# VectorE's order in the differential attention: a step's maximum ahead of the output of three steps ago and of the last product

## The chip, the cores and the metric

The kernel runs on one core of a Trainium2 chip. The metric is the device time of one execution in microseconds, the median of several runs; less is better. Four engines compute: TensorE (PE, its weight loads apart as PEld), VectorE (DVE), ScalarE (ACT) and GpSimd (POOL). Each works through its own list of instructions in the order in which the program gives them, and they wait for each other at semaphores.

## What is computed

Two blocks of two layers each stand one after the other, on 512 positions of width 1024, in float32. In each of the first two layers three mixers run side by side over the same normalised input: a neighbourhood attention, a differential attention with four heads, and a convolution. The change touches the differential attention alone:

```python
def blk(qs):
    a, b = qs
    s1 = jnp.einsum('bqhd,bkhd->bhqk', a, k1).astype(jnp.float32) * scale
    s2 = jnp.einsum('bqhd,bkhd->bhqk', b, k2).astype(jnp.float32) * scale
    w = jax.nn.softmax(s1, axis=-1) - lam * jax.nn.softmax(s2, axis=-1)
    return jnp.einsum('bhqk,bkhe->bqhe', w.astype(v.dtype), v)
...
def _diff_merge(o, subln_g, lam_init):
    return (_rms(o, subln_g) * (1.0 - lam_init)).reshape(o.shape[0], o.shape[1], -1)
```

The result is multiplied by a gate and goes into the layer's output projection. 512 latent positions attend to 768 keys (512 latent and 256 of a context). In the first layer the 256 context positions are queries too, and they attend to the 256 context keys alone. The second block (feed-forward layers, a recurrent mixer, a stick-breaking attention) follows and is the longer part of the time.

## The kernel before, in words

Each first-block layer has an `NaStage` (neighbourhood attention) and then a `LateStage` (convolution, differential attention). Once its projections are done, `LateStage` runs a loop over steps. A step is one head and one block of 128 queries. The first layer has 4 x 6 = 24 steps: four heads, each with four latent blocks (768 keys, "full" here) and then two context blocks (256 keys, "short"). The second layer has 4 x 4 = 16 steps, all full.

The work of step k, with the line that the profile gives for it:

- scores, TensorE (L345, 64-row operands): two maps of queries against keys, into one of two sets of three banks of PSUM
- max, VectorE (L1778, `max_dve`): the negated row maxima of both maps, straight from the banks (128x1536 values in a full step, 128x512 in a short one)
- exp, ScalarE (L1708, `exp_act`): two exponentials with their sums
- combine, VectorE (L1786, L1788, L1791, `combine_dve`): a reciprocal, a factor, and then map one minus lambda times map two
- turn, TensorE (L354, 128x128): transposes, two tiles into bank 7 and, in a full step, four into bank 6
- copy, ScalarE (L1695, and L1699 in a full step): out of the banks
- values, TensorE (L345, 128x96): the product with v, into bank 6
- o, VectorE (L1760, `o_dve`): out of bank 6, times the reciprocal of a sum
- root, ScalarE (L1684, L1686, L1688) and norm, VectorE (L1766, `norm_dve`): the RMS norm
- back, TensorE (L354, 128x96): a transpose into bank 7
- fin, VectorE (L1772, `fin_dve`): times the gate

The order on each engine is written out by hand, one line per engine and pass k of its loop, and is skewed over the steps:

- TensorE: values(k-3), back(k-4), turn(k-2), scores(k+1)
- ScalarE: root(k-3), copy(k-2), exp(k)
- VectorE: o(k-3), fin(k-4), max(k), combine(k-1), norm(k-3)

Four waits tie these lists together around the change. max(k) waits for scores(k). o(k-3) waits for values(k-3). turn(k-2) waits for fin(k-4), because bank 7 must be read before it is written again, and its second half waits for o(k-3), because of bank 6. scores(k+1) waits for exp(k-1), which reads the same banks. GpSimd and the DMA queues have nothing to do in the loop except to hold weights that were fetched before.

Of the kernel before, what the change touches and what calls it, by code (L numbers as in the profile page):

```python
# [190 lines left out]
def build(nc, ins, out_dram):  # L191
# [6 lines left out]
    with ctx:  # L198
# [240 lines left out]
        class Norm:  # L439
# [36 lines left out]
            def dve(self, q, e):  # L476
                for s in range(len(spans(self.total))):
                    q.wait_ge(*at(self.tag, "x", "rstd", s))
                    for i, j, c0, c1 in self.each(s):
                        if i >= 3:  # L480
                            q.wait_ge(*at(self.tag, "hi", i - 3))
                            q.wait_ge(*at(self.tag, "lo", i - 3))
                        e.scalar_tensor_tensor(self.full[i % 3][:, 0:c1 - c0], X(j, s), self.gain(j, s),
                                               self.squares.rs[:, c0:c1], MUL, MUL).then_inc(
                            *sig("norm_full", self.tag, "full", i))
                        if i:
                            self.lo(q, e, i - 1)
                self.lo(q, e, i)
# [903 lines left out]
        class LateStage:  # L1392
# [332 lines left out]
            def dve(self, q, e, drain):  # L1725
                self.conv_dve(q, e)
                taps = self.taps(q, e)
                for _ in range(self.taps_at[0]):
                    next(taps, None)
                self.mod_dve(q, e, 1)  # L1730
                for _ in range(self.taps_at[1]):
                    next(taps, None)
                some = lambda n: lambda i: [next(taps, None) for _ in range(n)]
                self.rope_dve(q, e, self.k_of, "k", some(self.taps_at[2]))
                self.v_of.dve(q, e, some(self.taps_at[3]))
                self.mod_dve(q, e, 2)
                self.rope_dve(q, e, self.q_of, "q", some(self.taps_at[4]))
                for _ in taps:
                    pass
                self.ln_dve(q, e)  # L1740
                self.mod_dve(q, e, 3)
                self.ln_gated(q, e)
                for k in range(self.n + 4):
                    if 3 <= k < self.n + 3:
                        self.o_dve(q, e, k - 3)
                    if k >= 4:
                        self.fin_dve(q, e, k - 4)
                    if k < self.n:
                        self.max_dve(q, e, k)
                    if 1 <= k <= self.n:  # L1750
                        self.combine_dve(q, e, k - 1)
                    if 3 <= k < self.n + 3:
                        self.norm_dve(q, e, k - 3)
                    drain(q, e, k - self.n)
# [1722 lines left out]
```

## Time and profile before

| | us |
|---|---|
| median of 3 runs (lowest, highest) | 3408.81 (3407.46, 3411.09) |
| the profiled execution | 3408.95 |
| its span in the profile | 3407.2 |
| busy: TensorE, VectorE, ScalarE, GpSimd | 3203.2, 1675.6, 1212.0, 715.3 |
| first layer's loop, from its first max to the last fin | 457.7 to 567.7 |
| second layer's loop, likewise | 968.4 to 1049.6 |

The profile is of one execution. Its page gives busy time by engine, the span in 40 slices, the chain of work that ended last, and groups of instructions by line. The trace behind it gives each instruction's start and length. In a row of the timeline the first number is the start in us from the beginning of the span, the second the length, then the engine, the line, the operation and its operands; x12 means that twelve such were merged into the row, and square brackets hold the idle time of the engine before it and what ended that. A matrix product of float32 takes two passes, so twice as many instructions are shown as the code has products.

### The profile page before, as it was taken

To read this page: it belongs to the slowest core of one execution; us is meant where nothing else is said; L and a number is where in the kernel's file an instruction comes from. 1 tells how busy PE (TensorE), PEld (TensorE's weight loads), DVE (VectorE), ACT (ScalarE), POOL (GpSimd) and SP (SyncE) were. 2 spreads that over 40 slices of the span, in tenths; PEclk is the share of its full clock that TensorE was granted. 3 is DMA by queue.
4 is the path that set the end of the run, shared out by engine and by line. 5 is a ranking of instruction groups with operands and counts; after the bars stand their busy time and mean duration, and the time that the engine had idled before them with its cause. 6 is when DMAs were issued, how large, how long until landed. Compare 5 with 4: busy or idle time off the path is not lost.

```text
span 3407.2 us, 40024 instructions
## 1 busy us (share of the span) xinstructions
PE 3203.2 (94%) x16252; PEld 2527.6 (74%) x16252; DVE 1675.6 (49%) x2558; ACT 1212.0 (36%) x2068; POOL 715.3 (21%) x518
## 2 busy tenths in 40 slices
PE   6999988899988999989899999999999999999998
PEld 4777766677866788867788778887888776578886
DVE  2155555415764634457655553446444525564344
ACT  3242165434264322233344332224222325542222
POOL 3204312331513100046332300001000343230000
PEclk9999999999999999999899999999999999999999
DMA  5303210121102233222000133222232231022322
GB/s 225 118 20 115 88 41 24 49 97 47 56 28 78 81 93 105 88 89 93 19 7 1 50 103 108 93 93 87 87 105 87 81 111 38 1 87 93 107 86 80
DMA packets 77575, 260.55 MB, mean 76 GB/s; under 512 B 8400, under 2 KB 9552, under 8 KB 76240
## 3 DMA queue, kind: packets, MB, share of 16 engines
q1 hardware_dynamic: 76528, 253.28, 22.6%
q0 software_dynamic: 864, 4.72, 0.4%
q8 instruction: 129, 2.11, 0.3%
q14 instruction: 54, 0.44, 0.0%
HBM read 255.87 MB, written 2.10 MB: 76 GB/s over the span
## 4 chain that ended last, share of the span: by engine, by line
PE 86%; DVE 7%; ACT 4%; POOL 1%; issue 1%; DMA 1%; SPq 0%; ACTq 0%; DVEq 0%; POOLq 0%
PE banks L345 85%; PE banks L354 1%; POOL w_lo L336 1%; DVE area L576 1%; DVE x_lat L579 1%; DMA area<-in_w_mod 1%; DVE small L1778 0%; DVE area L1722 0%; DVE area L1760 0%; ACT area L434 0%; POOL w_late L336 0%; ACT area L437 0%; ACT w_hi L326 0%; POOL area L410 0%; DVE area L494 0%
## 5 line engine op out<-in xcount | busy, mean ns | idle before, releaser
L345 PE MATMUL banks<-area,w_hi 128*128 128x512 f32 (+4 forms) x5896 | 1770.5, 383 | 24.0 <-POOL w_lo L336 8.1
L345 PEld LDWEIGHTS banks<-area,w_hi 128*128 128x128 f32 (+2 forms) x5896 | 1078.8, 188 | 288.4 <-issue 24.2
L345 PE MATMUL banks<-area,w_lo 128*128 128x512 f32 (+4 forms) x2948 | 1120.2, 381 | 0.0
L345 PEld LDWEIGHTS banks<-area,w_lo 128*128 128x128 f32 (+2 forms) x2948 | 554.8, 188 | 119.1
L345 PE MATMUL banks<-area,w_late 128*128 128x512 f32 (+2 forms) x2316 | 579.1, 399 | 28.8 <-ACT area L532 14.8
L326 ACT ACTIVATE w_hi<-w_raw 128x1024 fp32r<-128x1024 f32 (+2 forms) x361 | 349.5, 971 | 544.9 <-PE banks L345 413.4
L345 PEld LDWEIGHTS banks<-area,w_late 128*128 128x128 f32 (+1 forms) x2316 | 434.6, 190 | 146.3 <-ACT area L532 18.1
L345 PE MATMUL banks<-area,area 128*128 128x64 f32 (+10 forms) x3896 | 468.6, 326 | 71.7 <-DMA area<-in_w_mod 17.5
L345 PEld LDWEIGHTS banks<-area,area 128*128 128x128 f32 (+4 forms) x3896 | 384.0, 183 | 157.7 <-issue 71.9
L410 POOL TENSOR_TENSOR area<-area,area 128x512 f32<-128x512 f32 (+1 forms) x102 | 139.6, 1371 | 1475.2 <-ACT area L395 1473.4
L336 POOL TENSOR_TENSOR w_lo<-w_raw,w_hi 128x1024 fp32r<-128x1024 f32 (+1 forms) x133 | 308.7, 2323 | 455.4 <-ACT w_hi L326 455.4
L336 DVE TENSOR_TENSOR w_lo<-w_raw,w_hi 128x1024 fp32r<-128x1024 f32 (+1 forms) x228 | 263.2, 1155 | 158.7 <-ACT w_hi L326 158.7
L969 ACT ACTIVATE area<-area 128x512 fp32r<-128x512 f32 x88 | 55.6, 632 | 417.7 <-DVE area L1000 417.7
L326 ACT ACTIVATE w_late<-w_raw 128x1024 fp32r<-128x1024 f32 (+2 forms) x103 | 100.9, 979 | 235.9 <-PE banks L345 232.8
L345 PE MATMUL banks<-area,const 128*128 128x512 f32 (+4 forms) x422 | 149.2, 500 | 28.4 <-POOL area L410 8.2
L997 DVE TENSOR_TENSOR area<-banks,area 128x512 f32<-128x512 f32 x80 | 55.2, 691 | 239.1 <-PE banks L345 239.1
L1722 DVE SCALAR_TENSOR_TENSOR area<-area,par,area 128x783 f32<-128x783 f32 (+1 forms) x120 | 149.1, 1302 | 0.0
L862 DVE COPY area<-banks 128x512 f32<-128x512 f32 x72 | 46.9, 661 | 195.4 <-PE banks L345 179.1
L345 PEld LDWEIGHTS banks<-area,const 128*128 128x128 f32 (+3 forms) x422 | 69.4, 193 | 80.5 <-issue 33.7
L336 DVE TENSOR_TENSOR w_late<-w_raw,w_late 128x1024 fp32r<-128x1024 f32 (+1 forms) x76 | 86.1, 1133 | 85.4 <-ACT w_late L326 85.4
L989 DVE TENSOR_TENSOR area<-banks,area 128x512 f32<-128x512 f32 x80 | 55.3, 691 | 105.0 <-PE banks L345 105.0
L354 PE MATMUL banks<-const,area 128*128 128x128 f32 (+1 forms) x438 | 72.3, 284 | 33.9 <-DVE area L1772 21.4
(236 smaller groups left out, 2274.6 us busy)
## 6 DMA issues: line engine op xcount, KB each, us to landing
w_raw<-in_l_ffn_w_in SPq DMA_DIRECT2D x176, 512.0 KB, 3.2
w_raw<-in_l_ffn_w_out SPq DMA_DIRECT2D x128, 384.0 KB, 3.1
w_raw<-in_w_in SPq DMA_DIRECT2D x66, 512.0 KB, 3.5
w_raw<-in_w_mod SPq DMA_DIRECT2D x32, 512.0 KB, 5.4
w_raw<-in_w_qkv SPq DMA_DIRECT2D x24, 512.0 KB, 3.2
w_raw<-in_l_w_in SPq DMA_DIRECT2D x22, 512.0 KB, 3.3
w_raw<-in_w_out SPq DMA_DIRECT2D x32, 320.0 KB, 2.9
area<-in_w_mod SPq DMA_DIRECT2D x8, 1024.0 KB, 16.6
```

The lines of the kernel that those rows point to most:

```text
L326: e.activation(split_bufs(m)[0], raw_of(m), ACT.Copy).then_inc(*sig("w_rounded", "weights hi", m))
L336: e.tensor_tensor(lo, raw_of(m), hi.bitcast(f32), SUB).then_inc(*sig("w_split_dve" if dve else "w_split", "weights", m))
L345: return e.matmul(out, lhsT, rhs, start=first, stop=stop, skip_group_check=True)
L354: return e.transpose(out, in_, ident[0:k, 0:k])
L410: e.tensor_tensor(a, a, self.slot_of(s, j)[:, 0:c1 - c0], ADD).then_inc(*sig("squares_added", *self.tag, "added", s, j))
L576: e.scalar_tensor_tensor(y, y, self.gain(j, s), self.squares.rs[:, c0:c1], MUL, MUL).then_inc(*sig("post_step", self.tag, "step", s, j))
L579: e.tensor_tensor(x, x, y, ADD).then_inc(*sig("x_new", self.tag, "x", s, j))
L862: e.tensor_copy(yy, b).then_inc(*sig("evicted_dve", "evicted", u))
L969: e.activation(self.a_hi[:, j, :], a, ACT.Copy).then_inc(*sig("a_hi", self.tag, "a hi", half, j))
L989: e.tensor_tensor(sg, bank, self.norm.rs, MUL).then_inc(*sig("evicted_dve", "evicted", u))
L997: e.tensor_tensor(a, bank, self.norm.rs, MUL).then_inc(*sig("evicted_dve", "evicted", u))
L1722: e.scalar_tensor_tensor(yy, uu, w, yy, MUL, ADD).then_inc(*sig("taps", self.tag, "tap", m, k))
```

## The change

In the loop of `LateStage.dve` the call of `max_dve(q, e, k)` moves from the third place to the first. VectorE's list of pass k becomes max(k), o(k-3), fin(k-4), combine(k-1), norm(k-3). No instruction is added, taken out or changed, and no wait: each keeps the waits that it had. The lists of the other engines stay.

```diff
@@ -1741,12 +1741,12 @@
                 self.mod_dve(q, e, 3)
                 self.ln_gated(q, e)
                 for k in range(self.n + 4):
+                    if k < self.n:
+                        self.max_dve(q, e, k)
                     if 3 <= k < self.n + 3:
                         self.o_dve(q, e, k - 3)
                     if k >= 4:
                         self.fin_dve(q, e, k - 4)
-                    if k < self.n:
-                        self.max_dve(q, e, k)
                     if 1 <= k <= self.n:
                         self.combine_dve(q, e, k - 1)
                     if 3 <= k < self.n + 3:
```

## Rows read from the trace of the kernel before

**Rows 1.** Chain of waits, second layer, one full step: start, length, engine, line.

```profile
1018.50 0.32 DVE area L1760
...
1019.22 0.85 PE banks L354 x6
1020.07 3.02 PE banks L345 x24
```

**Rows 2.** Timeline of the same step, VectorE and TensorE's weight loads.

```profile
1018.74 0.34 DVE L1772 SCALAR_TENSOR_TENSOR area<-banks,small,area 96x128 f32<-96x128 f32 x1
...
1018.99 1.75 DVE L1778 TENSOR_REDUCE small<-banks 128x2 f32<-128x1536 f32 x1
...
1019.19 0.64 PEld L354 LDWEIGHTS banks<-const,area 128*128 128x128 f32 x6 [0.84 <-issue]
...
1020.00 1.16 PEld L345 LDWEIGHTS banks<-area,area 64*128 64x128 f32 x12 [0.17 <-issue]
...
1020.66 0.15 DVE L1786 RECIPROCAL small<-small 128x2 f32<-128x2 f32 x1
...
1021.49 1.41 PEld L345 LDWEIGHTS banks<-area,area 128*128 128x128 f32 x12 [0.33 <-issue]
...
1023.11 0.32 DVE L1760 TENSOR_SCALAR area<-banks,small 128x96 f32<-128x96 f32 x1 [0.81 <-PE banks L345]
```

**Rows 3.** Timeline of the second layer's first passes.

```profile
972.14 1.57 PE L345 MATMUL banks<-area,area 64*128 64x256 f32 x12 [2.46 <-ACT area L1708]
...
973.75 1.76 DVE L1778 TENSOR_REDUCE small<-banks 128x2 f32<-128x1536 f32 x1 [0.16 <-PE banks L345]
...
974.45 1.16 PEld L345 LDWEIGHTS banks<-area,area 64*128 64x128 f32 x12 [0.17 <-issue]
...
975.87 1.02 DVE L1791 SCALAR_TENSOR_TENSOR area<-area,small,area 128x768 f32<-128x768 f32 x1
...
977.57 0.32 DVE L1760 TENSOR_SCALAR area<-banks,small 128x96 f32<-128x96 f32 x1 [0.68 <-PE banks L345]
```

**Rows 4.** Timeline of the first layer: o's of one head's passes (one o left out).

```profile
505.51 0.32 DVE L1760 TENSOR_SCALAR area<-banks,small 128x96 f32<-128x96 f32 x1 [2.41 <-PE banks L345]
...
508.79 0.32 DVE L1760 TENSOR_SCALAR area<-banks,small 128x96 f32<-128x96 f32 x1
...
512.67 0.31 DVE L1760 TENSOR_SCALAR area<-banks,small 128x96 f32<-128x96 f32 x1
...
517.55 0.32 DVE L1760 TENSOR_SCALAR area<-banks,small 128x96 f32<-128x96 f32 x1 [0.81 <-PE banks L345]
...
525.46 0.32 DVE L1760 TENSOR_SCALAR area<-banks,small 128x96 f32<-128x96 f32 x1 [1.20 <-PE banks L345]
```

**Rows 5.** Timeline of the first layer: a short turn with the scores behind it.

```profile
506.20 0.20 PEld L354 LDWEIGHTS banks<-const,area 128*128 128x128 f32 x2 [0.84 <-issue]
...
506.57 1.16 PEld L345 LDWEIGHTS banks<-area,area 64*128 64x128 f32 x12 [0.17 <-issue]
```

**Rows 6.** Timeline of the first layer: a fin that waited, and the max behind it.

```profile
513.17 0.35 DVE L1772 SCALAR_TENSOR_TENSOR area<-banks,small,area 96x128 f32<-96x128 f32 x1 [0.18 <-PE banks L354]
...
513.43 1.74 DVE L1778 TENSOR_REDUCE small<-banks 128x2 f32<-128x1536 f32 x1
```

**Rows 7.** Timeline of the first layer's first passes.

```profile
465.53 1.17 PEld L345 LDWEIGHTS banks<-area,area 64*128 64x128 f32 x12 [0.17 <-issue]
...
466.51 1.02 DVE L1791 SCALAR_TENSOR_TENSOR area<-area,small,area 128x768 f32<-128x768 f32 x1
...
468.64 0.32 DVE L1760 TENSOR_SCALAR area<-banks,small 128x96 f32<-128x96 f32 x1 [1.12 <-PE banks L345]
```

**Rows 8.** Waits from 466 to 557 us: total, times, longest.

```profile
ACT area L1708 <- DVE small L1778: 3.4, 6, 0.7
```

**Rows 9.** Busy us (instructions) of PE, PEld, DVE, ACT, POOL; then clock, DMA share, GB/s.

```profile
460.00:466.00 6.00, 4.59 (x22) 3.41 (x24) 4.13 (x5) 3.86 (x10) 0.00 (x0) 0.56 0.01 1
...
974.00:1032.00 58.00, 50.67 (x399) 40.64 (x398) 47.27 (x87) 46.56 (x126) 0.00 (x0) 1.00 0.00 1
```

## The prediction

> **What bounds the kernel now.** I read the page first, to see where L1778, L1760 and L1772 (max, o and fin) stand on the chain that ended last. The page gives them little of the span, so the change lives in two short stretches, the two loops, and everything outside them is the same program. The next view is the chain of waits inside the second layer's loop [rows 1]: o, fin, turn, then scores and values as one run of 24 matrix instructions, then the next o. max is not in it. The timeline of the same step [rows 2] shows why: max begins right behind fin, while TensorE turns and scores, and VectorE is idle again for 0.81 us before the next o. From the starts the loop is: o to fin 0.24, fin to turn 0.45, turn to scores 0.81, scores to values 1.49, values to o 1.62; sum 4.61 us, which is the distance of the two o's (1018.50 and 1023.11) [rows 1, 2]. So the bound is a ring through two engines, and not one engine's work. The o closes it, because fin stands behind o on VectorE and turn waits for fin.
>
> In the first layer the steps are uneven [rows 4]. The distances of the o's there are 3.28, 3.88, 4.88 and twice 3.96 (517.55 to 525.46 is two passes), and the sixth pass is a full one of about 4.6 as above, together 24.55 us for one head. There are four heads, and the first three of them have all six passes with scores still to be made.
>
> **The change, part by part.** Nothing is added or removed, so the price of the instructions is zero. What moves is 40 max (24 and 16). No DMA, no GpSimd and no SyncE instruction is issued by it or passed by it. What the move adds is a wait in a new place: max(k) can't begin before scores(k) is complete, and o(k-3) and fin(k-4) are queued behind it on VectorE. For fin waits the turn, and for the turn all of TensorE's list. What it takes away is o and fin from in front of max.
>
> When do the scores end? The one row before in which max waited for steady scores says: the product began at 972.14 and max at 973.75, thus 1.61 us [rows 3]. How long does max hold VectorE? From its start to the next instruction's, 1.67 us (1018.99 to 1020.66) [rows 2]; I take 1.66, since 1.74 and 1.75 are its lengths and an instruction behind it begins some 0.08 before its end, as fin does behind o [rows 1, 2].
>
> The full step. Today o begins 1.49 + 1.62 = 3.11 us after the scores begin. With max in front it begins no sooner than 1.61 + 1.66 = 3.27. In other words, max has 1.5 us between the end of the scores and the end of the values, and needs 1.66. The other terms of the ring (0.24, 0.45, 0.81) stay. New ring: 4.77, so +0.16 us; I take +0.15, since the starts are rounded. The bounds of this small difference: 0.10 if max begins a few hundredths sooner, 0.25 if o starts only at the end of max's 1.75 instead of before it. combine and norm don't enter: in today's loop they start behind max, in the new one right behind fin, and 1.4 us plus norm end long before the next scores do.
>
> Second layer. The start first: max(3) is now ahead of o(0). VectorE is free at 975.87 + 1.02 - 0.08 = 976.81, the scores begun at 974.45 end at 976.06, so max runs from 976.81, and o(0) begins at 978.47 in place of 977.57 [rows 3]: +0.90. Then the o of steps 1 to 12 each pay the +0.15, 12 x 0.15 = 1.8. From o(13) on there is no max left in front. Sum 2.7 us.
>
> First layer. At the start TensorE is slower, so the scores begin at 465.53, and end about 467.14. VectorE is free at 466.51 + 0.94 = 467.45, max(3) holds it to 469.11, and o(0) was at 468.64 [rows 7]: +0.47. Then three heads with scores behind every turn. The two passes whose turn is full and whose scores are full take the new 4.76. The two passes that turn a short step but score a full one are another matter. Their turn is 0.37 in place of 0.81 [rows 5], and their values are short too, so today the ring is not bound by max and values but passes in 3.28 and 3.88 [rows 4]. In the new order they can't pass below 0.24 + 0.45 + 0.37 + 1.61 + 1.66 = 4.33. The two passes with short scores stay at 3.96 each: there max covers 512 values a row in place of 1536 and is done before values end, since those wait for ScalarE's copies. New head: 2 x 4.76 + 2 x 4.33 + 2 x 3.96 = 26.10, against 24.55: +1.55. For three heads 4.65; the fourth has no full scores behind its turns. Sum 0.47 + 4.65 = 5.1 us. One gain is in this already: 4.88 becomes 4.76, because max no longer stands between fin and norm.
>
> Together 2.7 + 5.1 = 7.8 us. Both loops end in TensorE's and ScalarE's work that hangs on the last steps, so the delay is passed on whole; behind them the output projection waits for the last fin. It is 3408.95 + 7.8 = 3416.75 for the profiled execution, and 0.14 less on the median, thus **3416.7 us**, +0.23%.
>
> A rule is to be weighed here, since the sum rests on nothing passing a waiting max. A row shows it: fin waited 0.18 us for TensorE, and the max behind it, whose scores had long been there, began only after it, at 513.43 [rows 6]. The Trainium skill (PSUM — Partial Sum Buffer, Engine vs sequencer instructions) says that these queues are strict first in, first out; by that the trace agrees. If an o could pass a waiting max, the sum would be zero.
>
> **The rivals.**
>
> *Faster: ScalarE gets its maxima sooner.* Today exp waited six times for max in the first layer, 3.4 us in all [rows 8]. The mechanism: in the passes with short turns VectorE is the late engine, and max first would start exp at once, and so free the banks for the next scores. If all of it came back and o lost nothing, the time would be 3408.95 - 3.4 = 3405.5. It decides only if max fits into the time that values take, so if it were shorter than 1.5 us, against 1.66. Also scores(k+1) waits for exp(k-1), not for exp(k), and those were early. Chance 0.06.
>
> *The same: the wait is hidden.* TensorE is the busiest engine of the loop, 50.67 of 58 us, VectorE has 47.27 [rows 9]. If the queue of TensorE had enough ahead, a late o would cost nothing, 3409. Half of it is the case where the 0.15 of the full steps vanishes but the short turns still pay: 24 x 0.15 less, about 3413 (24 being 12 + 6 full and 6 short turns). Against both: TensorE's list is a ring with the turn, and it sits idle before each turn already. Chance 0.14.
> The Trainium skill (Perfetto Trace Analysis, Identifying the Most-Contended Engine) says to optimise the engine of the highest occupancy first; read as a forecast, a move on VectorE would then leave the time as it is, which is this rival. The trace speaks against it, as the ring goes through both engines.
>
> *Much slower: TensorE's clock falls.* The granted clock is 1.00 in the loop, the higher level (2.4 GHz), and 0.56 between 460 and 466 us, after TensorE had waited for the first exp [rows 9]. With more idle time in each step it might fall to 1.2 GHz in the loops; if scores and values (3.1 of 4.6 us) took twice as long, a step would cost 3 us more and 36 steps 110 us, 3525. A tenth of that is 3428. The added idle is only 0.15 us on most steps and about 1 us on six. Chance 0.03. Other unforeseen delays of max in its new place (it now runs beside values and exp, not beside turn and scores), to 3423: chance 0.03.
>
> That the change isn't carried out is no rival: VectorE takes its list in program order.
>
> **How the numbers follow.** The forecast has a chance of 0.74. Its own range comes from the bounds of the full step's term (0.10 to 0.25 on 12 + 6 passes, -0.9 to +1.8 us) and of the four starts of 0.1 us around it, with the spread of the three runs (3407.5 to 3411.1): 3414 to 3420. To leave out no more than 2 in 10 the range reaches down to the half-hidden case: 3411.5 to 3420.5. A measurement of this kernel can tell about 0.2%, 6.8 us, from no change, and the limit for slower is thus 3415.6. Of the forecast's 0.74 three quarters or somewhat more lie above it, 0.57, and with the two dearer cases 0.06 it is slower 0.63; the rest of the forecast and the hidden case give the same 0.31; faster 0.06.
>
> **What would show it.** In the changed kernel: o's in the second layer 4.76 apart in place of 4.61, and L1778 on the chain of waits once in each full step, between scores and o; VectorE idle ahead of max, waiting for TensorE, and not ahead of o. In the first layer o's 4.3 apart where they were 3.28 and 3.88; the six waits of exp for max gone. max's own length unchanged at 1.74. Both loops later at their end by 5.1 and 7.8 us, and nothing changed outside. The prediction is wrong if max is found to end before values do, if o starts well behind max's end, or if the loops' clock isn't 1.00.

## The result

The changed kernel takes 3422.83 us (median of 5 runs, 3419.05 to 3424.27), and the kernel before, measured again beside it, 3407.95 (3407.10 to 3411.09). The ratio is 1.0038, with a 95% interval of 1.0024 to 1.0052: 14.9 us slower, where 7.8 were forecast. The direction was right. The size was outside the range, whose upper end was 3420.5.

The profiled execution took 3420.95 us, with a span of 3419.2 where the one before had 3407.2. The page of the changed kernel, with L1778 (max) now named in the chain by lines:

```profile
span 3419.2 us, 40024 instructions
...
PE 3213.1 (94%) x16252; PEld 2533.1 (74%) x16252; DVE 1674.3 (49%) x2558; ACT 1209.6 (35%) x2068; POOL 715.4 (21%) x518
...
PE banks L345 83%; DVE small L1778 1%; PE banks L354 1%; DVE area L576 1%; POOL w_lo L336 1%; DVE x_lat L579 1%; DMA area<-in_w_mod 1%; DVE area L1722 0%; DVE area L538 0%; ACT area L434 0%; DVE area L1760 0%; POOL w_late L336 0%; ACT area L437 0%; ACT w_hi L326 0%; DVE area L494 0%
```

The chain of waits in the second layer's loop, which answers to [rows 1] and [rows 2]:

```profile
1018.33 0.23 DVE area L1760
1018.55 0.25 DVE area L1772
...
1018.95 0.85 PE banks L354 x6
1019.80 1.52 PE banks L345 x12
...
1021.34 1.76 DVE small L1778
```

The run of 24 matrix instructions is cut to the 12 of the scores, and max has taken the place of the values. The timeline has the same passes:

```profile
1016.57 1.76 DVE L1778 TENSOR_REDUCE small<-banks 128x2 f32<-128x1536 f32 x1 [0.98 <-PE banks L345]
1018.24 0.31 DVE L1760 TENSOR_SCALAR area<-banks,small 128x96 f32<-128x96 f32 x1
...
1021.34 1.76 DVE L1778 TENSOR_REDUCE small<-banks 128x2 f32<-128x1536 f32 x1 [0.97 <-PE banks L345]
1023.02 0.31 DVE L1760 TENSOR_SCALAR area<-banks,small 128x96 f32<-128x96 f32 x1
```

VectorE now waits 0.97 us for the scores ahead of max and not at all ahead of o. The o's are 4.77 or 4.78 us apart (1018.24 to 1023.02), where they were 4.61.

The first layer, the o's of the same head as in [rows 4], and TensorE around its long pass:

```profile
505.78 0.31 DVE L1760 TENSOR_SCALAR area<-banks,small 128x96 f32<-128x96 f32 x1
...
510.12 0.31 DVE L1760 TENSOR_SCALAR area<-banks,small 128x96 f32<-128x96 f32 x1
...
515.71 0.31 DVE L1760 TENSOR_SCALAR area<-banks,small 128x96 f32<-128x96 f32 x1
```

```profile
510.83 0.41 PE L354 MATMUL banks<-const,area 128*128 128x128 f32 x2 [1.71 <-DVE small L1786]
511.17 3.81 PE L345 MATMUL banks<-area,area 64*128 64x256 f32 x16
...
514.03 1.76 DVE L1778 TENSOR_REDUCE small<-banks 128x2 f32<-128x1536 f32 x1 [1.79 <-PE banks L345]
```

The turn waits for fin; the rows name L1786 as the releaser because it stands right behind fin and ends last (fin at 510.69 us, L1786 at 510.75, the turn begins at 510.83).

510.12 less 505.78 is 4.34 us, as worked out. The next pass has the same work and takes 5.59. In it the scores run slower: 3.81 us for the 16 merged instructions, which take 2.18 in the first head, at 485.08 us. The stretches of the timeline give the clock, before and after; the columns are those of [rows 9].

Before:

```profile
500.00:525.00 25.00, 20.48 (x152) 15.54 (x152) 19.30 (x42) 18.79 (x59) 0.00 (x0) 1.00 0.00 1
525.00:550.00 25.00, 20.48 (x151) 15.39 (x150) 19.30 (x42) 18.70 (x58) 0.00 (x0) 1.00 0.01 2
```

After:

```profile
475.00:500.00 25.00, 18.39 (x138) 14.01 (x139) 19.26 (x42) 18.23 (x58) 0.00 (x0) 1.00 0.00 1
500.00:525.00 25.00, 19.02 (x133) 14.40 (x132) 17.20 (x39) 16.17 (x52) 0.00 (x0) 0.93 0.00 1
525.00:550.00 25.00, 19.39 (x133) 14.47 (x133) 18.07 (x39) 16.37 (x55) 0.00 (x0) 0.93 0.00 1
510.90:511.30 0.40, 0.40 (x4) 0.23 (x6) 0.36 (x2) 0.37 (x2) 0.00 (x0) 1.00 0.00 0
511.40:514.70 3.30, 3.30 (x16) 2.34 (x15) 1.51 (x3) 2.08 (x5) 0.00 (x0) 0.50 0.00 0
```

In the first head TensorE was idle for 1.71 us ahead of two turns in a row (484.74 and 489.08), where the idle time ahead of a turn had been 0.53 to 0.65, and the clock stayed at 2.4 GHz. In the second head it fell to 1.2 GHz between 511.30 and 511.40 us, thus behind the first of the two idle stretches, which had ended at 510.83; the second one, ahead of the turn at 516.42, came later and was 1.32 us. The third head has the same, with the idle stretch up to 538.17 and the clock at 0.50 from 538.70 on.

Where the 12.0 us between the two spans lie, by the starts of the first max and of the last fin of each loop:

| us | before | after | difference |
|---|---|---|---|
| up to the first max | 457.70 | 455.81 | -1.89 |
| first layer's loop | 109.64 | 118.48 | +8.84 |
| between the loops | 401.08 | 400.18 | -0.90 |
| second layer's loop | 80.84 | 84.40 | +3.56 |
| behind | 2357.94 | 2360.33 | +2.39 |

The first line is scatter: nothing ahead of the first max is changed, and in the executions below without spare work it begins anywhere from 454.4 to 457.5 us.

### The profile page after: what moved, and what is told of

The parts are those of the page before. It is cut to its first block, busy times and chain, and to the rows that moved or that the text cites. A ratio compares the mean times of both kernels' runs of the same rounds, so it can differ in the third digit from the quotient of the medians.

```text
span 3419.2 us, 40024 instructions
## 1 busy us (share of the span) xinstructions
PE 3213.1 (94%) x16252; PEld 2533.1 (74%) x16252; DVE 1674.3 (49%) x2558; ACT 1209.6 (35%) x2068; POOL 715.4 (21%) x518
## 4 chain that ended last, share of the span: by engine, by line
PE 85%; DVE 8%; ACT 4%; POOL 1%; issue 1%; DMA 1%; SPq 0%; ACTq 0%; DVEq 0%; POOLq 0%
PE banks L345 83%; DVE small L1778 1%; PE banks L354 1%; DVE area L576 1%; POOL w_lo L336 1%; DVE x_lat L579 1%; DMA area<-in_w_mod 1%; DVE area L1722 0%; DVE area L538 0%; ACT area L434 0%; DVE area L1760 0%; POOL w_late L336 0%; ACT area L437 0%; ACT w_hi L326 0%; DVE area L494 0%
## 5 line engine op out<-in xcount | busy, mean ns | idle before, releaser
L345 PE MATMUL banks<-area,area 128*128 128x64 f32 (+10 forms) x3896 | 476.0, 332 | 69.5 <-DMA area<-in_w_mod 15.6
L336 POOL TENSOR_TENSOR w_lo<-w_raw,w_hi 128x1024 fp32r<-128x1024 f32 (+1 forms) x133 | 308.5, 2322 | 454.5 <-ACT w_hi L326 454.4
```

The lines of the kernel that those rows point to most:

```text
L336: e.tensor_tensor(lo, raw_of(m), hi.bitcast(f32), SUB).then_inc(*sig("w_split_dve" if dve else "w_split", "weights", m))
L345: return e.matmul(out, lhsT, rhs, start=first, stop=stop, skip_group_check=True)
```

## The experiments

Two theories stood against each other for the 7 us that the forecast lacked. One: the ring was priced rightly, and the rest is TensorE's clock, which falls in the loop because the new order leaves TensorE idle longer, and elsewhere because everything comes later. The other: the new order costs more than the ring, or the falls are chance. Medians are quoted with those of the kernel before on the same chip.

### The kernel before, again

> The kernel before, once more, beside itself; its own profile shows what is the same from one execution to the next. Ring theory (the new time is the longer ring of max, o, fin and turn, plus drops of TensorE's clock where the new order leaves TensorE idle longer): ratio 1.000, both loops as before, 109.6 us from first max to last fin in the first layer and 80.8 in the second, clock 1.00 in the passes from 475 to 550 us. Rival, chance (the clock's drops fall anywhere from one execution to the next, whatever the order): this kernel too shows drops inside the first layer's loop, and the loop differs by 1 to 3 us from 109.6.

3407.21 us beside 3408.10, ratio 0.9997 (0.9988 to 1.0006). First loop 111.04 us, second 85.18, between them 399.42, behind 2356.93; 109.6 and 80.8 had been expected of the loops. The passes from o to o are those of before to 0.01 us, and the clock is 1.00 from 475 to 550 us. What differs is the starts and the ends. From the first max to the first o it took 12.04 us instead of 10.94 in the first loop and 10.71 instead of 9.14 in the second. The first loop's last pass took 6.34 instead of 6.06, and the second loop's last two 5.44 and 6.91 instead of 4.57 and 4.99, at a clock below 1.00. So one kernel's second loop can differ by 4.3 us from one execution to the next. A loop's length alone therefore says little; its passes say much.

### The changed kernel, again, and each layer alone

```diff
+                    if self.l == 1 and k < self.n:
+                        self.max_dve(q, e, k)
                     if 3 <= k < self.n + 3:
                         self.o_dve(q, e, k - 3)
                     if k >= 4:
                         self.fin_dve(q, e, k - 4)
-                    if k < self.n:
+                    if self.l != 1 and k < self.n:
                         self.max_dve(q, e, k)
```

This is the run with the order of the change in the second layer only, as a diff to the kernel before with its two other lines in place; the run with the first layer only has 0 in place of 1.

> The changed kernel, once more. Ring theory with the order as cause of the clock's drops: first loop 117 to 119 us again, with one pass of about 5.6 us in place of 4.34 in most heads where two short turns follow each other, clock under 1.00 there; second loop 83.6 to 84.4 us; ratio about 1.003 to 1.004. Rival, chance: no drops in this execution, first loop 114.8, second 83.5, and ratio 1.002.

> max ahead of o and fin in the second layer only. Ring theory: the first loop as before (109.6 us), the second longer by 2.7 us, up to 3.6 if its start falls on a low clock; o's 4.77 us apart; in all +2.7 to +3.6, ratio 1.001. Rival (part of the extra time is made outside the loops, by the shift of everything behind): +5 us or more, with the surplus outside both loops.

> max ahead of o and fin in the first layer only. Ring theory with the clock's drops caused by the order: first loop +7.5 to +9 us (5.1 of ring, the rest clock), second loop as before, o's there 4.61 us apart; in all +7.5 to +9, ratio 1.0025. Rival, chance: +5.1 us, ratio 1.0015, with the first loop at 114.8.

| | median us | of before | ratio (95%) | first loop | second loop |
|---|---|---|---|---|---|
| changed, again | 3422.57 | 3408.10 | 1.0036 (1.0024 to 1.0049) | 118.54 | 86.32 |
| second layer only | 3411.07 | 3408.10 | 1.0006 (0.9997 to 1.0015) | 110.98 | 85.77 |
| first layer only | 3422.09 | 3408.10 | 1.0038 (1.0026 to 1.0051) | 118.55 | 83.48 |

The second layer alone costs 3.0 us in the median (interval -1.0 to 5.1), where 2.7 to 3.6 was expected; its o's are 4.77 apart. Its profiled second loop, 85.77, is longer than the 83.5 to 84.4 expected, and so is that of the changed kernel, 86.32; in the first it is the start (10.89 us for 9.14) and the last pass (6.39 for 4.99) that grew beyond the ring, in the second the last two passes (5.38 and 6.79 for 4.57 and 4.99). The first layer alone costs 14.0 (8.9 to 17.4), and 7.5 to 9 was expected. In its loop that came true: 118.55 us, 8 more than the 109.6 to 111.0 of the unchanged order. The other 6 us lie outside the loop, which neither theory's expectation had. All three profiled executions with the new order in the first layer have the same picture there: short-turn passes of 4.34, and one of 5.59 to 5.71 in the second and in the third head. The rival "chance" is out for these two falls: in the seven profiled executions that have the old order in the first layer (before, before again, second layer only, fin ahead of o, and the three delays below), no pass there between the loop's first and last is longer than 4.88 us, whenever the loop began.

### Spare work in TensorE's idle stretches

```diff
                     if k >= 4:
                         self.back_pe(q, e, k - 4)
+                    if k + 1 < self.n and self.keys(max(k - 3, 0)) == TC:
+                        self.filler_pe(q, e, k + 1)
...
+            def filler_pe(self, q, e, k):
+                h_, i = self.steps[k]
+                q.wait_ge(*at(self.tag, "exp", k - 2, 1))
+                for _ in range(4):
+                    mm(e, self.scores(k)[:, 0, 0:256], self.qd[0:64, h_, i * P:(i + 1) * P],
+                       self.kd[0:64, h_, T:TA], True, True)
```

> The changed kernel, and in the first layer TensorE makes four spare products of 64x128 by 64x256 into the banks of the coming scores (which overwrite them) in the two passes of each head whose values are short, where it is idle for 1.7 us in the changed order. Theory (the clock falls because of those idle stretches): clock 1.00 from 475 to 550 us, the o's there 4.34 apart in all heads and none 5.6, first loop shorter than the changed kernel's 118.5 us by 2.5, so 116; ratio 1.003 or less. Rival (the clock's drops come at any place with the shifted times): still two passes of 5.6 us, and the first loop at 118.5 or more.

3419.21 us beside 3408.01, ratio 1.0029 (1.0020 to 1.0038). No pass of 5.6 us is left, but four products were too many for the idle time: the passes became 4.66 to 4.70 and 5.10 instead of 4.34 and 4.78, and the first loop took 116.56. So I ran it with two (range(2)).

> As the run with four spare products, with two in each of those passes, about 1 us of work into an idle stretch of 1.7, so that they cost nothing themselves. Theory (idle stretches of the changed order make the clock fall): clock 1.00 from 475 to 550 us and all short turn passes at 4.34 and the next at 4.34, first loop 115 to 116 us (118.5 in the changed kernel, 110 to 111 before); ratio 1.002 to 1.003. Rival: two spare products don't hold the clock, and passes of 5.6 us come back.

3415.34 us beside 3407.48, ratio 1.0022 (1.0013 to 1.0031). The rows of TensorE and of the clock in the head where the changed kernel lost 1.25 us:

```profile
506.68 0.41 PE L354 MATMUL banks<-const,area 128*128 128x128 f32 x2 [0.82 <-DVE small L1795]
...
511.02 0.41 PE L354 MATMUL banks<-const,area 128*128 128x128 f32 x2 [0.46 <-DVE small L1795]
...
515.35 0.85 PE L354 MATMUL banks<-const,area 128*128 128x128 f32 x6 [0.50 <-DVE small L1795]
```

```profile
475.00:500.00 25.00, 20.62 (x147) 15.18 (x145) 19.16 (x42) 18.04 (x57) 0.00 (x0) 1.00 0.00 1
500.00:525.00 25.00, 20.77 (x151) 15.63 (x151) 18.38 (x41) 17.35 (x56) 0.00 (x0) 1.00 0.01 2
525.00:550.00 25.00, 20.77 (x148) 15.39 (x148) 18.34 (x41) 17.38 (x55) 0.00 (x0) 1.00 0.00 1
```

The idle time ahead of the turns is 0.5 us in place of 1.7, the clock is 1.00, every short-turn pass takes 4.34 or 4.33, and the last pass, which had taken 6.06 before and 7.33 in the changed kernel, takes 4.80, with the clock at 1.00 there too. The loop took 113.45 us, less than the 115 expected. The order of VectorE is the changed one, word for word, and the work on TensorE is more; the kernel is 6.6 us faster for it (+7.9 us to the kernel before, where the changed one has +14.5). Its eleven executions took 3410.8 to 3420.2 us; nine of the ten of the changed kernel took 3419.1 to 3424.3, and one 3414.5.

That +7.9 comes out next to the forecast's 7.8 is in part luck: its interval is 4.4 to 10.6, and in the profiled execution the first loop's last pass is 1.3 us shorter than in the kernel before, while the second loop's last two are 2.6 longer (5.59 and 6.59 for 4.57 and 4.99). The passes at the full clock are the better check. From the first o to the last but one, the first loop took 93.20 us for 88.60, thus +4.60; from the first o to the fourteenth, the second took 60.67 for 58.69, thus +1.98.

### The delay without the new order

```diff
+                if self.l == 0:
+                    for _ in range(25):
+                        mm(e, self.scores(0)[:, 0, 0:256], self.qd[0:64, 0, 0:P], self.kd[0:64, 0, T:TA], True, True)
                 self.scores_pe(q, e, 0)
                 for k in range(self.n + 4):
```

> The kernel before with its order, and 25 spare products on TensorE ahead of the first scores of the first layer's loop, some 9 to 11 us of TensorE at work and nothing else changed. It tells the shift of everything behind from the change of order. Theory (what the changed kernel loses outside its first loop comes only from the clock's drops, which differ with when work falls): the time from the first max on is as before in the first loop (109.6 to 111.0), and all of it outside that loop may be up to 4 us longer than the delay put in. Rival (the surplus outside is a cost of the new order in the second loop and behind): outside the first loop nothing beyond the delay, within 1 us.

> The kernel before with 13 spare products ahead of the first layer's loop (25 gave a delay of 7.7 us and a total of +10.9). Delay 2.5 us by 0.43 us a product. Theory (the surplus behind comes from when the work falls against the clock's drops): total +0 to +5, the surplus not in proportion to the delay. Rival (each us of delay brings 0.4 us of surplus): +3.5.

> The same with 40 spare products: delay 14.1 us. Theory: total between +12 and +18, the surplus not in proportion. Rival (0.4 us of surplus per us of delay): +20.

The delay is how long VectorE waited ahead of the first max in the profiled execution, 7.66 us with 25 products; in the kernel before it did not wait there:

| products | delay us | median us | of before | more than the delay | span of the profiled run less the delay |
|---|---|---|---|---|---|
| 13 | 2.5 | 3413.91 | 3407.48 | +3.9 | 3411.2 |
| 25 | 7.7 | 3418.93 | 3408.01 | +3.2 | 3411.6 |
| 40 | 14.1 | 3427.10 | 3407.48 | +5.5 | 3403.6 |

With the old order, a mere delay also costs 3.2 to 5.5 us more than itself in the medians. Each one by itself is weak: by the intervals of the ratios the surplus is 0.9 to 7.0 us with 13 products, -2.9 to 4.3 with 25 and -1.5 to 7.0 with 40, so only the first is clear of nothing. Whether it is in proportion to the delay isn't settled: 0.4 per us would be 1, 3 and 6, which these intervals still allow, though the medians, 3.9, 3.2 and 5.5, don't rise that way. Both ends missed the totals that were expected (+6.4 where 0 to 5 was said, +19.6 where 12 to 18 was said and the rival said 20). The first loop itself took 109.7 to 110.8 us in the three, as with no delay. Single executions scatter: with 40 products two of the five runs were 3418.4 and 3419.4, and the profiled one of them was 3.6 us below before once the delay is taken off.

The surplus goes with the clock again. The changed kernel and the one with 25 products begin their second loop at the same time, 974.47 and 974.50 us. Between the two loops their work, some 7 us later than before, has one more fall of the clock in it. Before:

```profile
640.00:700.00 60.00, 50.48 (x221) 35.74 (x220) 34.60 (x64) 30.88 (x51) 10.52 (x6) 0.94 0.18 62
```

The changed kernel, and then the old order with 25 products, both 7 us later, with the same 34.60 us of VectorE:

```profile
647.00:707.00 60.00, 51.54 (x225) 36.66 (x224) 34.60 (x64) 30.80 (x51) 10.53 (x6) 0.91 0.18 62
```

```profile
647.00:707.00 60.00, 51.63 (x225) 36.67 (x224) 34.60 (x64) 30.82 (x51) 10.52 (x6) 0.91 0.17 62
```

0.91 against 0.94 of 60 us is 2 x 0.03 x 60 = 3.6 us more at 1.2 GHz. One fall more doesn't lengthen every stretch, though: between the loops these two took 400.18 and 400.22 us, and the kernel before 401.08. For the whole execution the same sum can be made: twice (1 minus the granted clock) times the length, over the whole span. Set against the span without what the queues explain (2.7, 5.1 or 7.8 us of ring, or the delay put in):

| profiled run | us at 1.2 GHz | span less ring or delay |
|---|---|---|
| two spare products a pass | 130 | 3405.4 |
| second layer only | 133 | 3405.3 |
| 40 products | 133 | 3403.6 |
| before, before again | 143, 144 | 3407.2, 3408.2 |
| 13 products, 25 products | 153, 157 | 3411.2, 3411.6 |
| changed again, changed | 167, 170 | 3413.4, 3411.4 |
| first layer only | 174 | 3415.7 |

A straight line through the ten has 0.23 us per us at the low level, some 10 us from the top of the table to the bottom, and all ten lie within 3 us of it, whatever their order on VectorE. The same holds with the kernel held fixed: the record gives time and granted clock of 183 executions, and against the mean of its own kernel and chip each us at 1.2 GHz goes with 0.23 us of time (correlation 0.81). This is a correlation; no run sets the clock outside the loops by itself. In the first loop the granted clock is 0.91 in all three profiled executions with the changed order there, 0.95 before and 0.97 with two spare products.

### A shorter maximum

```diff
-                e.reduce_max(st[:, 2:4], self.scores(k)[:, :, 0:self.keys(k)], X_AXIS, negate=True).then_inc(
+                e.reduce_max(st[:, 2:4], self.scores(k)[:, :, 0:min(self.keys(k), 512)], X_AXIS, negate=True).then_inc(
```

> The changed order, with max over the first 512 of the 768 keys of each map (128x1024 values in place of 128x1536, part of the maximum is left out), so about 1.2 us in place of 1.75. Overrun theory (max costs what it takes beyond the 1.5 us between the end of the scores and of the values): second layer's o's back at 4.61 us, VectorE again idle before o; short turn passes 3.9 in place of 4.34, first loop within 1 to 2 us of before; ratio 1.000. Rival (max in front costs a fixed handshake of 0.16 us in each pass, whatever its length): o's stay 4.77 apart in the second layer.

This kernel leaves a third of the keys out of the maximum.

```profile
1014.37 1.23 DVE L1778 TENSOR_REDUCE small<-banks 128x2 f32<-128x1024 f32 x1 [0.97 <-PE banks L345]
1015.87 0.32 DVE L1760 TENSOR_SCALAR area<-banks,small 128x96 f32<-128x96 f32 x1 [0.27 <-PE banks L345]
...
1020.48 0.32 DVE L1760 TENSOR_SCALAR area<-banks,small 128x96 f32<-128x96 f32 x1 [0.27 <-PE banks L345]
```

max is still in front, but fits: VectorE waits 0.27 us for the values again, and the o's are 4.61 apart. The short-turn passes take 3.81 and 3.80 (3.28 and 3.88 before, 4.34 in the changed kernel), and the first loop 109.67 us. Median 3407.22 beside 3408.01, ratio 0.9996 (0.9988 to 1.0005). In a full step being in front costs nothing; the overrun does.

### max between o and fin

```diff
                 for k in range(self.n + 4):
-                    if k < self.n:
-                        self.max_dve(q, e, k)
                     if 3 <= k < self.n + 3:
                         self.o_dve(q, e, k - 3)
+                    if k < self.n:
+                        self.max_dve(q, e, k)
                     if k >= 4:
                         self.fin_dve(q, e, k - 4)
```

> The order o, max, fin, combine, norm in both layers: max behind o, but ahead of fin. Ring theory (fin releases the turn, so all of max lies in the ring): full passes 4.61 + 1.66 = 6.27 us, second loop +20 us, first loop +22 us, ratio 1.012. Rival (what costs is the late o, through its reader on ScalarE and the values): o is on time here, and the loops stay within 3 us of before.

```profile
1032.46 0.32 DVE L1760 TENSOR_SCALAR area<-banks,small 128x96 f32<-128x96 f32 x1 [4.11 <-PE banks L345]
1032.69 1.75 DVE L1778 TENSOR_REDUCE small<-banks 128x2 f32<-128x1536 f32 x1
1034.36 0.34 DVE L1772 SCALAR_TENSOR_TENSOR area<-banks,small,area 96x128 f32<-96x128 f32 x1
...
1038.73 0.32 DVE L1760 TENSOR_SCALAR area<-banks,small 128x96 f32<-128x96 f32 x1 [2.47 <-PE banks L345]
```

```profile
480.00:500.00 20.00, 13.27 (x64) 9.18 (x62) 10.65 (x21) 9.64 (x28) 0.00 (x0) 0.61 0.00 1
```

The pass of 6.27 us is there to the hundredth (1032.46 to 1038.73): fin closes the ring. But most full passes of the second loop take 7.9 or 9.2: TensorE is idle for longer still, and its clock falls again and again (0.61 in the stretch shown, 0.78 over the first loop and 0.77 over the second). Median 3498.2 beside 3408.01, ratio 1.0262 (1.0248 to 1.0276): 90 us, where the ring alone gave 42. The first loop took 154.0 us, the second 124.5. What the ring leaves over, 48 us, is more than the ring.

### fin ahead of o

```diff
+                    if self.l == 1 and k >= 4:
+                        self.fin_dve(q, e, k - 4)
                     if 3 <= k < self.n + 3:
                         self.o_dve(q, e, k - 3)
-                    if k >= 4:
+                    if self.l == 0 and k >= 4:
                         self.fin_dve(q, e, k - 4)
```

> The kernel before, and in the second layer fin(k-4) ahead of o(k-3) on VectorE, max behind both. Ring theory (the ring is closed by fin, and back is ready 1.67 us after the values begin): passes of 4.44 us in place of 4.61, second loop 1 to 2 us shorter than 80.8 on the same clock; total -1, within what can be told. Rival (o closes the ring, through its reader on ScalarE): passes longer than 4.61.

```profile
1004.08 0.35 DVE L1774 SCALAR_TENSOR_TENSOR area<-banks,small,area 96x128 f32<-96x128 f32 x1 [0.69 <-PE banks L354]
1004.34 0.30 DVE L1762 TENSOR_SCALAR area<-banks,small 128x96 f32<-128x96 f32 x1
...
1008.57 0.35 DVE L1774 SCALAR_TENSOR_TENSOR area<-banks,small,area 96x128 f32<-96x128 f32 x1 [0.69 <-PE banks L354]
```

The passes are 4.49 us, shorter than 4.61 as the ring says, if less than worked out (4.44). Eleven such passes gain 1.3 us; the one ahead of them (4.45 for 4.07) and the one behind (4.21 for 3.93) lose 0.7 of it, and the second loop's end fell on the low clock (last two passes 5.24 and 6.93, against 4.57 and 4.99). Median 3409.40 beside 3407.48, ratio 1.0005 (0.9996 to 1.0014): no difference that can be told. No version here that computes the same beats the kernel before.

## Why the prediction was right, and where it was wrong

**The bound.** Right. It is a ring over two engines, closed by fin: max between o and fin gave 6.27, fin ahead of o gave 4.49, both on the side that the ring says.

**The full step**, +0.15 us from an overrun of 1.66 over 1.5. Right: 4.77 or 4.78 against 4.61, so +0.16 to 0.17, and zero when max was shortened. The 1.61 from scores to max and the 1.67 from max to the next instruction were read from one row each and held.

**The short-turn steps**, 3.28 and 3.88 to 4.33. Right where the clock was at 2.4 GHz: 4.34 and 4.34; a head 26.09 for the 26.10 of the sum (474.91 to 501.00). The starts, +0.47 and +0.90, were +0.46 and, in the second layer, +1.74: there o(0) came at 985.36 - 974.47 = 10.89 after the first max in place of 9.15, with the first passes on a low clock (0.72 from 978 to 984 us). In the changed kernel's other execution it was 10.06, +0.91. The first layer's +0.46 holds against this one execution of before; with the old order that start took 10.56 to 12.04 us from one execution to the next. The run with the second layer alone, and 3.0 us in its median, doesn't contradict 2.7.

**The sum**, 7.8. The ring's part of it is right: in the run with two spare products the passes at the full clock give +4.60 in the first layer, where 4.65 was worked out, and +1.98 in the second, where 1.8 was; the starts add some 1.4. That its median comes out at +7.9 is in part luck, as said there.

**The step that failed** is the clock rival, "TensorE's clock falls", with a chance of 0.03. The sum put the clock's cost at nothing, and the prediction named a clock below 1.00 in the loops as a sign of being wrong. It was 0.93 in two of the stretches above. The one row of a low clock that the prediction had, 460 to 466 us, was read a little late: TensorE was idle from 455.9 to 461.4 us, and the clock fell within that idle time (1.00 up to 458.4, 0.50 from 459 to 465), not behind it. The rival was priced for falls in every step (3525) or a tenth of that (3428), and it was put aside because the added idle is "only 0.15 us on most steps and about 1 us on six". That size was right: 1.71 us for 0.53 to 0.65. What was wrong is that about 1 us on six steps was taken to cost nothing. Those six are three pairs of neighbours, and it is there, in the first of a pair, that the clock fell. From the prediction's own numbers the idle time could be had: a pass of 4.33 us in which TensorE has 0.37 of turn, 1.5 of scores and under a microsecond of short values and back leaves about 1.5 us. No case of the clock between the forecast and 3428 had a price. It cost:

- In the loop, two passes of 5.59 and 5.62 in place of 4.34: 2.5 us, and as much or 0.2 more in the two other profiled executions with this order and no spare work. Shown, by the spare products.
- At the loop's end, the last pass 7.33 in place of 6.06: 1.3 us. It goes with the place in time as well, as the old order has 7.40 there with 25 products and 7.47 with 40.
- Outside the first loop some 3 us, with a spread of the same size from one execution to the next. This is what is left of the 14.9 and 14.5 of the two comparisons once 7.8 and the two items above are taken off, and no measurement of its own. The delays with the old order bring 3.2 to 5.5.

The first item is shown as a cause. That the surplus outside goes with time on the low clock is shown by the table and by the 183 executions; that the clock causes it is argued. Why a later time should make more falls likely, whether the surplus follows the size of the delay, why the first head has no fall, and the part of the first-layer run's 6 us that is more than 3, stay open.

The Trainium skill (TensorE: Matmul & The Clock Gate, A second HAM failure mode: psum-queue depth-cycling) says of one measured kernel that short idle gaps between groups of matrix products came often enough there for the clock to go back and forth between its levels. With that the trace agrees: the longest gap in the loop's middle ahead of these falls was 1.71 us, and the clock went from 1.00 to 0.50 and back.

**The other rivals.** "Faster" had the waits of exp for max right: the six are gone from the first layer's loop, with one new wait of 1.8 us at its start, and it brought nothing, as nobody waited for exp. "The same" is out by the passes. The busiest engine was no guide here: between 500 and 525 us TensorE went from 20.48 to 19.02 us of work while the passes grew. It isn't even clear which engine that is; from 974 to 1032 us before, TensorE has 50.67 us of matrix products but 40.64 of weight loads, and VectorE 47.27.

## What to carry to other kernels

In a loop of hand-ordered queues, find the ring and not the busiest engine: list for each wait how long after its release the waiting instruction may begin, and an instruction put in front costs what it overruns (here 0.16 us of 1.75 in a full step). Then work out how long TensorE stands idle in the new ring, pass by pass, and give the clock a term of its own with a middle value: the same idle time costs twice, once as waiting and once as matrix work at 1.2 GHz. Read passes, not lengths of loops, where the ends of the loops fall on a low clock by chance.

## What the runs showed of the hardware that was not expected

- In each of three profiles of the new order the clock fell to 1.2 GHz in the second and in the third head, 0.3 to 0.5 us behind the end of an idle stretch of TensorE of 1.71 us, the longest in the loop's middle. In the first head two such stretches, 4.3 us apart, brought no fall; with stretches of 0.5 us in their place (two spare products) there was none in any head.
- Spare matrix work of 1.1 us in each of six passes, into banks that are overwritten, made the changed kernel 6.6 us faster (+7.9 for +14.5, each against the kernel before beside it), 5 of them in the loop.
- Time goes with the granted clock at 0.23 us per us at 1.2 GHz, from one execution of the same kernel to the next (183 executions) as between the kernels here.
- A delay alone, with no other change, came out 3.2 to 5.5 us dearer than itself in three medians, of which only the one with 13 products is clear of the noise.
